# Copies behind five kinds of TensorE chores, issued one turn of the gather loop later on ScalarE

## The reference

```python
q = (xn @ w_q).reshape(B, S, 8, 2, 64)                   # 8 heads, two halves
s = jnp.einsum('bshpd,hpkd->bshpk', q, sub_keys)         # scores against 128 sub-keys a half
...                                                      # top 16 of each half, then top 16 of their sums
experts = i1 * 128 + i2                                  # 8 x 16 = 128 experts a token, out of 16384
g = softmax(top_s)
u = expert_u[ec]                                         # a row of 1024 for each token and expert
act = gelu(einsum('cd,ced->ce', xc, u))
out = einsum('ce,ced->cd', g * act, expert_v[ec])
```

## Time and profile before

| | |
|---|---|
| median of 3 runs | 1251.49 us (1250.04 to 1252.54) |
| profiled execution | 1249.78 us, its span 1248.0 us |
| TensorE matmuls busy | 1063.3 us (85%) |
| VectorE busy | 795.7 us (64%) |
| ScalarE busy | 454.8 us (36%) |
| gathers | 268.45 MB in 256 instructions |
| all transfers | 432.08 MB, mean 346 GB/s |

### The profile page before, as it was taken

How to read it: one execution, slowest core, us unless ns; L and a number is a source line. 1 busy time by engine, 2 the same in 40 slices (tenths; PEclk the granted TensorE clock), 3 DMA queues, 4 the chain that set the end, 5 groups by cost and what they waited for, 6 DMA issues and landing times.

```text
span 1248.0 us, 13843 instructions
## 1 busy us (share of the span) xinstructions
PE 1063.3 (85%) x5002; PEld 532.2 (43%) x5002; DVE 795.7 (64%) x1865; ACT 454.8 (36%) x1256; POOL 290.0 (23%) x261
## 2 busy tenths in 40 slices
PE   6999986887786667669977799968998998999998
PEld 2888572432242113223432344423442444555543
DVE  5567758997755999763447667576655477645201
ACT  1132126654433444452353343435334423332201
POOL 0000013434333543623323333333332000000000
PEclk9998987998998999979999899998998999999999
DMA  9987419999999999999999999999999975444573
GB/s 390 408 336 311 179 63 372 366 375 418 420 351 422 421 421 419 412 418 391 421 420 421 421 421 420 421 421 397 421 422 421 361 269 203 160 159 151 206 297 124
DMA packets 63487, 432.08 MB, mean 346 GB/s; under 512 B 6931, under 2 KB 10300, under 8 KB 11836
## 3 DMA queue, kind: packets, MB, share of 16 engines
q0 software_dynamic: 36864, 268.45, 52.7%
q1 hardware_dynamic: 26160, 161.76, 32.6%
q10 hardware_dynamic: 396, 0.99, 0.2%
HBM read 430.12 MB, written 1.06 MB: 346 GB/s over the span
## 4 chain that ended last, share of the span: by engine, by line
PE 49%; DMA 22%; DVE 19%; ACT 6%; issue 2%; POOL 1%; SPq 0%; DVEq 0%; POOLq 0%
PE ps L1140 20%; DMA AR<-in_puv,idx 19%; PE ps L1095 10%; DVE AR L1722 7%; PE ps L771 4%; DMA W<-in_w_mod 3%; PE ps L990 2%; PE ps L1254 2%; PE ps L1035 2%; PE ps L1121 1%; POOL AR L2513 1%; DVE rowb L1867 1%; ACT av L2258 1%; DVE RT L1694 1%; PE ps L779 1%
## 5 line engine op out<-in xcount | busy, mean ns | idle before, releaser
L2513 POOL DMA_INDIRECT AR<-in_puv,idx x256 | 289.6, 1131 | 673.0 <-PE ps L1095 441.1
L1095 PE MATMUL ps<-AR,acc 128*64 128x512 f32 x904 | 276.3, 654 | 110.0 <-ACT acc L2137 108.8
L1722 DVE CUSTOM_DVE_ANT_0 AR<-AR,mixT 128x1024 f32<-128x1024 f32 x128 | 153.7, 1222 | 69.7 <-DMA AR<-in_puv,idx 69.4
L1140 PE MATMUL ps<-W,AR 128*128 128x512 f32 x416 | 188.5, 596 | 0.7 <-ACT AR L2137 0.7
L1095 PEld LDWEIGHTS ps<-AR,acc 128*64 128x64 f32 x904 | 70.0, 144 | 268.1 <-ACT acc L2137 176.6
L1722 DVE CUSTOM_DVE_ANT_0 AR<-AR,tok 128x1024 f32<-128x1024 f32 x128 | 152.8, 1219 | 41.1 <-DMA AR<-in_puv,idx 40.9
L1140 PE MATMUL ps<-W,hT 128*128 128x512 f32 x320 | 156.1, 618 | 5.4 <-DVE PT L2029 4.2
L2256 ACT ACTIVATE av<-av 128x1 f32<-128x1 f32 x256 | 51.2, 200 | 288.2 <-DVE av L1722 287.9
L1140 PEld LDWEIGHTS ps<-W,AR 128*128 128x128 f32 x416 | 75.6, 190 | 77.9 <-issue 75.8
L1140 PEld LDWEIGHTS ps<-W,hT 128*128 128x128 f32 x320 | 56.9, 194 | 80.4 <-issue 72.0
L2137 ACT ACTIVATE acc<-fold,av 128x64 f32<-128x64 f32 x226 | 78.6, 348 | 7.4
(11 more groups left out here) (459 smaller groups left out, 1306.5 us busy)
## 6 DMA issues: line engine op xcount, KB each, us to landing
W<-in_w_in SPq DMA_DIRECT2D x90, 1024.0 KB, 9.0
W<-in_w_mod SPq DMA_DIRECT2D x24, 1024.0 KB, 12.3
W<-in_wba SPq DMA_DIRECT2D x8, 1024.0 KB, 8.0
W<-in_wbb SPq DMA_DIRECT2D x8, 1024.0 KB, 8.3
W<-in_wo SPq DMA_DIRECT2D x8, 1024.0 KB, 6.9
W<-in_w_out SPq DMA_DIRECT2D x4, 1024.0 KB, 8.3
W<-in_wq SPq DMA_DIRECT2D x4, 1024.0 KB, 5.9
AR<-in_puv,idx POOLq DMA_INDIRECT x256, 13.0
```

The lines of the kernel that those rows point to most:

```text
L1095: t = mm(of(("E", a, c))[64 * g:64 * g + 64, :], dg_at((2 * p + g) % NDG, late), GB[:, places[g], D + c * 512:D + c * 512 + 512], start=(m ...
L1140: t = mm(b[:, :], src[:, k, :], slab(i)[:, k, :], start=(k == 0), stop=(k == 7))
L1722: ttr(GB[:, n, 0:D], GB[:, n, 0:D], H2[a][g], 1.0, 0.0, MUL, ADD, av[:, a, c:c + 1]).then_inc(*ve.sig("dot", p, g))
L2513: eng.indirect_dma_start(GB[:, n, :], None, puv, bass.IndirectOffsetOnAxis(ap=idx[:, a, c:c + 1], axis=0)).then_inc(*gp.dma(f"g{n}", "gat" ...
```

## The change

The ScalarE part of the five chores becomes a chore of its own (`q_copy`, `p_copy`, `cmp_copy`, `h_copy`, `h2_copy`). It isn't put into the list with the TensorE part, but kept back and put there at the next `flush_copies()`, which stands right behind `weight(p)` of each turn. So a copy behind a chore of turn p stands behind the weights of turn p + 1, ahead of the other chores of that turn. The counter `asked`, which says when the keys of a pair of heads may be asked for, goes up with the copy. Before the loop the four copies of q_back stand behind the first routing. The functions that issue the copies are the same.

```diff
+COPIED = {"q_project": "q_copy", "turn_p": "p_copy", "cmp_turn": "cmp_copy", "q_norm2": "h_copy", "q_back": "h2_copy"}
...
+    copies = []
+
     def do(*chore):
         out.append(chore)
-        if chore[0] == "q_project" and chore[3][-1] == 1:
-            asked[chore[1]] += 1
+        if chore[0] in COPIED:
+            copies.append((COPIED[chore[0]], *chore[1:]))
+
+    def flush_copies():
+
+        while copies:
+            chore = copies.pop(0)
+            out.append(chore)
+            if chore[0] == "q_copy" and chore[3][-1] == 1:
+                asked[chore[1]] += 1
...
     while (0, 0) not in idx or (0, 0) not in gw:
         advance(routes, 1)
+    flush_copies()
     do("conv_mix", 1)
     do("q_project", 0, 1, (0, 1))
+    flush_copies()
     do("gate2_cols")
...
             h2 = h2_next(h2)
+            flush_copies()
...
         do("weight", p, bool(state["late"]))
+        flush_copies()
         if a == 0:
             do("accumulate", p, places, bool(state["late"]))
...
-            parts = {"q_back": q_back, "q_project": q_project, "gexp": gexp, "weight": weight, "scores_add": scores_add,
-                     "cmp_s2": cmp_s2, "cmp_turn": cmp_turn, "turn_p": turn_p, "attn_root": attn_root, "q_norm1": q_norm1,
-                     "q_norm2": q_norm2, "spread_gate": spread_gate, "x2_add": x2_add, "x2_gain": x2_gain,
+            parts = {"h2_copy": q_back, "q_copy": q_project, "gexp": gexp, "weight": weight, "scores_add": scores_add,
+                     "cmp_s2": cmp_s2, "cmp_copy": cmp_turn, "p_copy": turn_p, "attn_root": attn_root, "q_norm1": q_norm1,
+                     "h_copy": q_norm2, "spread_gate": spread_gate, "x2_add": x2_add, "x2_gain": x2_gain,
```

## The result

The changed kernel took 1249.07 us (median of 20 runs, 1244.7 to 1254.5) and the kernel before, on the same chip, 1254.12 (20 runs, 1249.04 to 1259.18). The ratio is 0.9972, 95% interval [0.9961, 0.9984]: faster by 0.28%, 3.5 us, with 2.0 to 4.9 us inside the interval. The two medians lie 5.05 us apart, a little outside it; I go by the ratio, and two later comparisons of the same kernels gave 0.46 and 0.63%. The forecast was faster by 6.0 us. The direction is right and the size is not. The 1251.49 from which the forecast was counted was a median of three runs; larger sets of the same kernel later gave 1253.3 to 1255.7.

A forecast was written before the change was run, and what follows sets the result against it. It took the gather transfers at about 420 GB/s as the bound, with VectorE and a chain of waits causing two shortfalls. Terms -5.2 - 1.0 + 0 = -6.2, set as -6.0 from 1251.49: 1245.5 us, range 1241.5 to 1249.5.

The forecast's parts named there:

- The dip at turns 27 to 32: Loop at 345 to 370 us, 333 GB/s from a chain of waits: earlier weights let gathers run full, -5.2 us.
- The gain at turns 2 and 3: Gelu of turn 3 and gather of turn 6 come 3.6 us sooner; VectorE is the bound there, so only 1.5 us won.
- The holds: Turns 5 and 13: TensorE chores wait for PSUM banks freed by the moved copies; +0.5 us charged, nothing in turn 5.
- the stage's net of -1.0: VectorE-bound stretch, 189 to 290 us: gain of 1.5 less 0.5 for the bank waits, -1.0 us.
- the holds' upper end: Waits at turns 5 and 13 if neither is covered: 1.6 + 1.5 = 3.1 us lost.
- Before the loop: Four q_back copies go behind the first exponential while ScalarE has idle time: 0 charged, bound 1.9 us.
- The rest: Turns 28 to 53, other q_project copies and second-half q_back: gathers run full once the dip is over, hidden, 0.
- The base: Starting time of the kernel before, median 1251.49 us, from which the forecast's 6.0 us was taken off.
- half of it: Rival, 0.12: dip closes only partly because TensorE is still in q_project, VectorE stage gives nothing; -3, 1248.5 us.
- The rival that was slower: Chance 0.06: PSUM holds of turns 5 and 13 each cost a turn's gathers 5.0 us; +3.3, 1254.8 us.

The follow-up runs named there:

- e1: Against the kernel before, only the copies behind chores of turn 24 and later moved a turn on; 1248.85 us, ratio 0.9940.
- e8: The full change unaltered, measured and profiled once more against the kernel before; 1248.96 us, ratio 0.9954.
- e11: The kernel before with turn_p(4)'s two copies alone moved from turn 2 to turn 3; 1252.04 us, ratio 0.9989.
- e7: The kernel before with turn_p(5)'s copies alone moved a turn on; 1257.89 us, ratio 1.0026.
- e17: The full change plus thrown-away TensorE work: extra transposes in turn_p(5)'s first half, identity products at turn 10's accumulate; 1247.90 us, ratio 0.9951.
- e18: Second profile of the e17 kernel; no time given, gather of turn 28 at -2.3 us and turn 50 at -7.0 against the kernel before.
- e4: The full change with load_keys(1) moved from turn 9's chores to turn 15's, in effect the unaltered change; 1247.65 us, ratio 0.9937.
- e15: The full change unaltered, profiled once more; no time given, gather of turn 28 at +1.3 us and turn 50 at -3.7 against the kernel before.
- e9: The full change with the second key table's load made to wait for turn_p(7) instead of turn_p(6); 1249.71 us, ratio 0.9961.
- e16: The e5 kernel profiled once more; no time given, gather of turn 28 at +0.8 us and turn 50 at -4.2 against the kernel before.
- e2: Against the kernel before, only the copies of the front and of turns 2 to 13 moved a turn on; 1255.09 us, ratio 0.9985.
- e3: The full change with the copies of turns 5, 12 and 13 put back right behind their matmuls; 1247.56 us, ratio 0.9929.
- e5: The full change with turn_p(5)'s copies alone put back right behind their transposes; 1247.35 us, ratio 0.9946.

## Why the prediction was right in direction and wrong in size

- **The dip at turns 27 to 32, -5.2.** Right, with its mechanism: 420 GB/s, POOL idle 0.68 us where it was 6.73, -5.3 us by itself (e1), -5.4, -4.8, -2.8 and -5.0 in the four executions of the whole change. The -2.8 is e8's, which had issued its gathers 4.2 us sooner going in; in bytes it gained 5.0 us like the others (421 GB/s against 400 over 100 us).
- **The gain at turns 2 and 3, -1.5.** Right: the gelu of turn 3 goes at 209.04, 0.2 us behind its dot and 3.6 us sooner counted from the first gather, as reckoned; -5.0 at turn 6 (more than the 3.6 reckoned), -0.9 at turn 7, -1.8 at turn 20 in e11.
- **The holds, "I charge 0.5, and nothing in turn 5, where the earlier start covers the 1.5 us".** This is the term that failed, and with it the stage's net of -1.0. Less the gain of 1.5, the stage lost about 2.9 us in three executions of four (+1.3 to +1.6 at turn 28), near the 3.1 that I had set as the holds' upper end; in the fourth it won more than the forecast. The waits themselves were as reckoned: TensorE 2.33 and 0.69 us at turn 5, VectorE 2.35 us at take_g where 2.4 was said. Where the clock holds they are covered in this kernel (e8), as the forecast had it; alone, turn 5's costs 1.7 us at turn 9 (e7). What the forecast lacks is the clock: behind turn 5's idle stretch it went to half in two of these executions and not in the other two, at 2.5 us (e17 and e18 against e4 and e15), and in the same two once more behind turn 13's. In the third a gather landed late at turn 10, with no hold there, and the clock fell behind it; the forecast does not have that at all, and how its loss divides between landing and clock is open. I had reckoned each wait of TensorE as time in a queue, and read the clock column of the earlier trace rows without asking what work keeps it up.
- **Before the loop, 0.** Right: 16.85 and 16.88 us from norm_h's transposes to the first gather.
- **The rest, 0.** About right up to turn 63. At turn 64 the kernels with the late copies moved hand back 0.4 to 2.3 us of issue time (the change 1.6, 1.9, 2.3 and 1.9 from turn 50 to 64); the kernel before moves by 0.1 and 0.8 there. I did not try that place.
- **The base.** The four profiles of the change are 4.1 us under the first of the kernel before over the loop, on average (3.5, 4.8, 5.2, 3.0); the other two of the kernel before are 0.5 and 3.5 us over the first. The change's three comparisons, e4 counted as one, gave 0.28, 0.63 and 0.46%. Their mean weighted by the intervals is 0.38%, 4.8 us, though they scatter by more than the intervals; the one beside the forecast is the least of them. By all of them the forecast of 6 us is too high by 1 to 2 us.

Of the rivals, "half of it" names the size that came (-3) by the wrong mechanism: the dip closed in full, and the stage ahead of it lost. The rival that was slower named the right place, the PSUM holds at turns 5 and 13, with a price of 5.0 us for each missed place; the fall at turn 5 costs 2.5, and not always.

**What stays open.** Why gather 10's second half lands in 7.8 to 10.5 us in some executions and 10.8 to 11.8 in others (not the key table's load, e9; not turn 5's hold, e16), and whether a fill would help behind a late one. Why the clock near 9 us behind the first gather is 0.50 in some executions and 1.00 in others. And e2, e7 and e11 lose 2.2 to 2.8 us from turn 54 to 55, with TensorE idle for 2.58 us ahead of an accumulate that then takes 3.62 us for seven matmuls (e7 below), which none of the three profiles of the kernel before does; it looks like the same thing at a third place, but I filled nothing there.

```profile
482.74 1.10 PE L1068 MATMUL ps<-K,hT 128*64 128x128 f32 x15
486.42 3.62 PE L1113 MATMUL ps<-AR,acc 128*64 128x512 f32 x7 [2.58 <-ACT acc L2155]
```

No version was shown to be better than the change: e3 (1247.56), e5 (1247.35) and e17 (1247.90) lie 1.2 to 1.7 us under its 1249.07, but they were measured at other times and beside other runs of the kernel before, and e5 beside e8 on one chip is 1247.35 against 1248.96, within both intervals.

## What to carry to other kernels

Move a copy behind urgent work where the matmuls that need its bank come a turn later, and leave it at its place where the next chore takes the same bank: the first gave 5 us here, the second made TensorE idle. A stretch in which TensorE stands idle is not priced by its length alone when the work behind it is on the path: look at the durations of the same matmuls before and behind it, in the kernel before as well. And profile a changed kernel several times before explaining its loss: one execution of four had nothing of it.

## What the hardware showed that I had not expected

- The same idle stretch of TensorE (2.29 and 2.33 us, between the same instructions) was followed by full clock in one execution and by half clock in another, and with the half clock the gather of turn 9 came 3.1 us later (+1.8 against -1.3). The two had differed from 8.3 us behind the first gather on, in the granted clock (0.50 and 1.00) at the same work. An idle stretch of 2.3 us is not needed for it either: the kernel before falls at this place behind idle stretches of 0.69 us and less. The Trainium skill (TensorE: Matmul & The Clock Gate, Part 1) says that one kernel runs a different number of its matmuls at the low clock from run to run; the four profiles of the change agree, the three of the kernel before, alike up to turn 13, show no such difference there.
- Sixteen transposes whose results are thrown away, issued where TensorE stood idle at turn 5, kept the granted clock at 1.00 in both executions, and turn 9's gather came 2.4 to 2.5 us sooner than in the two executions that were alike up to there without them.
- Three profiles of the kernel before stand within 0.4 us of each other at turn 28 (though not at turn 127, +3.5). With a handful of copies of 0.4 to 0.6 us put elsewhere, four profiles of one kernel scatter by 5.8 us there (+1.6 to -4.2).
